# Transposed attention outputs, paired score heads, a transposed first projection and the softmax division on GpSimd, in a hybrid decoder layer with a 32-expert MoE

## The reference: what is computed

```python
h = rms_norm(x, g_mix)
rq, rk, rv, rg, mq, mk, mv, cq, gl = split(h @ w_in)     # 256x256, 256x256, 256x512 ... , 256x3072
o_ret  = rms_norm(retention(rq, rk * 64**-0.5, rv)) * silu(rg)   # 4 heads: causal scores times a decay, no softmax
o_moba = causal softmax attention of mq, mk, mv with ALiBi       # 8 heads of 64, q and k RMS-normed
o_mem  = softmax attention of cq into 256 memory tokens          # 4 heads of 128, keys ck and values cv from mem
y = gates0 * (o_ret @ w_br_ret) + gates1 * (o_moba @ w_br_moba) + gates2 * (o_mem @ w_br_mem)
x = x + y @ w_out
```

## Time and profile before

| | |
|---|---|
| median of 3 runs | 1211.34 us (1210.7 to 1211.85) |
| profiled execution, its own time | 1211.36 us |
| its span, first to last instruction | 1209.5 us |
| mean granted TensorE clock | 0.996 |
| PE busy | 1151.7 us (95%) |
| DVE busy | 410.5 us (34%) |
| ACT busy | 225.6 us (19%) |
| POOL busy | 8.7 us (1%) |
| bytes moved by DMA | 454.93 MB, mean 376 GB/s |

### The profile page before, as it was taken

The page is one execution under the profiler, slowest core; times in us unless marked ns, Lnnn a source line. Parts: engine busy times, 40 slices in busy tenths (PEclk is TensorE's granted clock), DMA queues, the critical chain, the costliest instruction groups (busy, mean ns, idle before and its releaser), DMA issues.

```text
span 1209.5 us, 13242 instructions
## 1 busy us (share of the span) xinstructions
PE 1151.7 (95%) x5401; PEld 536.6 (44%) x5401; DVE 410.5 (34%) x677; ACT 225.6 (19%) x344; POOL 8.7 (1%) x17
## 2 busy tenths in 40 slices
PE   8999999999999999999999999998999999899997
PEld 5888888874333333333433333333333333333332
DVE  4865656864222222222222222222222222222221
ACT  3544447441000000010100000000000000000001
POOL 0100000000000000000000000000000000000000
PEclk9999999999998999999999999999999999999999
DMA  9755454599999999999999999999999999999995
GB/s 352 255 181 169 157 171 157 183 374 429 427 426 423 413 427 429 426 430 424 430 427 429 427 428 428 427 428 429 427 429 427 427 428 430 426 429 426 429 428 237
DMA packets 52322, 454.93 MB, mean 376 GB/s; under 512 B 4368, under 2 KB 4400, under 8 KB 27504
## 3 DMA queue, kind: packets, MB, share of 16 engines
q1 hardware_dynamic: 50816, 449.69, 89.8%
q0 software_dynamic: 784, 2.38, 0.5%
q10 hardware_dynamic: 672, 2.10, 0.5%
HBM read 453.11 MB, written 1.05 MB: 375 GB/s over the span
## 4 chain that ended last, share of the span: by engine, by line
PE 58%; DMA 40%; DVE 1%; issue 1%; ACT 0%; SPq 0%; DVEq 0%; ACTq 0%
PE PS L1456 19%; DMA merge_raw<-in_w_mlp 14%; DMA prob_raw<-in_w_mlp 14%; DMA raw<-in_w_mlp 12%; PE PS L1462 9%; PE PS L1273 6%; PE PS L1275 5%; PE PS L1274 5%; PE PS L1492 3%; PE PS L1431 2%; PE PS L1290 1%; PE PS L1269 1%; PE PS L1438 1%; PE PS L1344 1%; PE PS L1444 1%
## 5 line engine op out<-in xcount | busy, mean ns | idle before, releaser
L1456 PE MATMUL PS<-raw,XG 128*64 128x512 f32 x544 | 123.0, 594 | 11.2 <-DMA raw<-in_w_mlp 11.2
L1185 DVE TENSOR_SCALAR hT<-PS 128x512 f32<-128x512 f32 x32 | 22.1, 692 | 317.7 <-PE PS L1456 317.7
L779 ACT ACTIVATE hT<-hT 128x512 f32<-128x512 f32 x31 | 19.5, 630 | 553.0 <-DVE hT L1185 553.0
L1456 PE MATMUL PS<-merge_raw,XG 128*64 128x512 f32 x480 | 107.5, 596 | 6.2 <-DMA merge_raw<-in_w_mlp 5.9
L857 DVE TENSOR_TENSOR rest<-raw,mix_hi 128x2048 fp32r<-128x2048 f32 x38 | 87.0, 2291 | 55.2 <-ACT mix_hi L631 55.2
L1116 DVE COPY XG<-PS 128x512 f32<-128x512 f32 x32 | 22.1, 692 | 229.0 <-PE PS L1438 229.0
L1123 DVE TENSOR_TENSOR X<-X,PS 128x512 f32<-128x512 f32 x120 | 74.4, 682 | 53.1 <-PE PS L1492 53.1
L1273 PE MATMUL PS<-mix_hi,hTh 128*128 128x512 f32 x224 | 89.8, 401 | 0.0
L1275 PE MATMUL PS<-mix_hi,hTl 128*128 128x512 f32 x224 | 88.2, 394 | 0.0
L1274 PE MATMUL PS<-rest,hTh 128*128 128x512 f32 x224 | 88.1, 393 | 0.0
L631 ACT ACTIVATE mix_hi<-raw 128x2048 fp32r<-128x2048 f32 x38 | 72.6, 1913 | 42.9 <-PE PS L1275 39.9
(11 more groups left out here) (272 smaller groups left out, 1246.8 us busy)
## 6 DMA issues: line engine op xcount, KB each, us to landing
raw<-in_w_mlp SPq DMA_DIRECT2D x48, 2048.0 KB, 34.1
merge_raw<-in_w_mlp SPq DMA_DIRECT2D x47, 2048.0 KB, 33.8
gate_raw<-in_w_mlp SPq DMA_DIRECT2D x24, 2048.0 KB, 32.5
value_raw<-in_w_mlp SPq DMA_DIRECT2D x24, 2048.0 KB, 32.7
hi_raw<-in_w_mlp SPq DMA_DIRECT2D x24, 2048.0 KB, 32.3
prob_raw<-in_w_mlp SPq DMA_DIRECT2D x24, 2048.0 KB, 33.8
raw<-in_w_in SPq DMA_DIRECT2D x24, 1024.0 KB, 5.1
raw<-in_w_mem_kv SPq DMA_DIRECT2D x4, 1024.0 KB, 5.1
```

The costliest lines, as they stand in the source:

```text
L1185: dve.tensor_scalar(glu, PS[:, 0:1024:2], LIMIT, None, ALU.min).then_inc(swi, 1)
L1456: mm = pe.matmul(PS[h * SL:(h + 1) * SL, n * 512:(n + 1) * 512], XG[:, 2 * u + c, :], tile[:, cols], start=False, stop=(u == W1U - 1 and c ...
```

## The change

- **First group transposed.** `rqk` now holds 128 x 128 blocks of the weights still and streams the 256 tokens of `hTf` by, with k in the outer loop and the four output blocks in the inner one, into four banks (0, 1, 4, 5). DVE copies q^T and k^T straight out; the `qT` tasks of `rqk` go. The row scale of x, which had been multiplied into q and k, is left off q and squared into the scale of `rv`; the retention norm takes a per-token epsilon in two square roots on ACT in place of one.
- **Scores in row halves.** `ret_s` and the moba `sc` treat two heads together, one in rows 0 to 63 of the array and one in rows 64 to 127, alternating matmul by matmul. The first 128 queries no longer get scores for keys 128 to 255, so `alibi`, the maxima and exp run over 128 + 256 columns; the maxima are negated by the reduction itself.
- **Softmax division on GpSimd.** POOL multiplies the probabilities in place by the reciprocals, two `tensor_scalar` instructions for a head, and `pT` waits for that (`norm_done`) and no longer for exp.
- **Outputs transposed.** `pv` holds V still and streams the transposed probabilities by, so it makes o^T: one task for two moba heads (each in half of the columns) or one mem head. ACT copies out the high part and DVE the remainder; the `oT` tasks of moba and mem go.
- Several SBUF tiles move, the second bias load and the router's loads on POOL come behind the first multiplications, and `b_mlp2` no longer waits for `oT`.

```diff
@@ rqk and its readers
-               "mq": tasks(*[("qT", "rqk", t) for t in tiles]),
+               "mq": [],
-                        for t in range(TT):
-                            ins = dve.tensor_scalar(tq[0][:, t, :], P2[:, t, :], rx[:, t:t + 1], None, ALU.mult)
+                        dve.tensor_tensor(rx_sq[:, :], rx, rx, ALU.mult).then_inc(rx_sq_done, 1)
+                        for c in (0, 2):
+                            b = RQK_BANKS[c]
+                            ins = dve.tensor_copy(qTs[g][:, c:c + 2, :],
+                                                  PS[:, 512 * b:512 * b + 1024].rearrange("p (c n) -> p c n", c=2)[:, :, 0:S])
+                    if g == "rqk":
+                        for k in range(KC):
+                            w = raw[k // 4][:, :].rearrange("p (k n) -> p k n", k=4)[:, k % 4, :]
+                            if k in PIECE_AT:
+                                pe.wait_ge(hTf_done, PIECE_AT.index(k) + 1)
+                            if k < 3:
+                                pe.wait_ge(first_w[k], 16)
+                            if k in (4, 6):
+                                pe.wait_ge(second_w[(k - 4) // 2], 16)
+                            for c in range(4):
+                                mm = pe.matmul(banks[RQK_BANKS[c]][:, 0:S], w[:, c * P:(c + 1) * P], hTf[:, k, :],
+                                               start=(k == 0), stop=(k == KC - 1))
@@ POOL
+            def normalised(h):
+                if HEADS[h][0] == "moba":
+                    pool.wait_ge(rcp_done, h + 1)
+                else:
+                    in_sbuf(pool, ("sc", h))
+                for it in range(TT):
+                    cols = SCORE_COLS[it] if HEADS[h][0] == "moba" else slice(it * S, (it + 1) * S)
+                    ins = pool.tensor_scalar(probs[h % 4][:, cols], probs[h % 4][:, cols], smx[:, 3, 2 * h + it:2 * h + it + 1], None, ALU.mult)
+                ins.then_inc(norm_done, 1)
...
-            for i in range(6):
+            for i in range(7):
                 if i == 2:
                     load_router(pool)
+                if i >= 1:
+                    normalised(2 * i - 2)
+                    normalised(2 * i - 1)
                 if i >= 2:
                     pool.wait_ge(pair_sem(f"gate{i - 2}"), GI[f"gate{i - 2}"] // 2 + 1)
+                if i == 6:
+                    continue
                 pool.dma_start(bg[:, i % 2, :], a["b_gate"][0:1, 512 * i:512 * i + 512].to_broadcast([P, 512])).then_inc(bias_in[i % 2], 16)
@@ ACT
-                        roots(f"ret{hp}", 2 * TT, RET_DV)
+                        head_roots(f"ret{hp}", 2, RET_DV)
+                    elif kind == "pv":
+                        br, c = key[1:]
+                        act.wait_ge(task_done, TASKS[key] + 1)
+                        act.activation(oTp[br][0][:, c, :], b[:, 0:S], ACT.Copy).then_inc(part_high, 1)
@@ DVE
-                        dve.scalar_tensor_tensor(src, alibi[:, :], 2.0 ** (-8.0 * (hh + 1) / MOBA_H), b, ALU.mult, ALU.add)\
+                        dve.scalar_tensor_tensor(src[:, 0:384], alibi[:, :], 2.0 ** (-8.0 * (hh + 1) / MOBA_H), b[:, 0:384], ALU.mult, ALU.add)\
+                        for it in range(TT):
+                            dve.tensor_reduce(smx[:, 1, 2 * h + it:2 * h + it + 1], src[:, SCORE_COLS[it]], AX.X, ALU.max, negate=True)\
+                                .then_inc(max_done, 1)
-                    dve.tensor_tensor(o[br][:, :, hh * hd:(hh + 1) * hd],
-                                      b[:, 0:TT * hd].rearrange("p (t d) -> p t d", d=hd),
...
+                    dve.wait_ge(part_high, PARTS.index(key) + 1)
+                    dve.tensor_tensor(oTp[br][1][:, c, :], b[:, 0:S], oTp[br][0][:, c, :].bitcast(F32), ALU.subtract).then_inc(done, 1)
@@ PE
+                    if br == "moba":
+                        pe.wait_ge(bank_read[(n + 1) % 4], (n + 1) // 4)
+                        heads = [(slice(64 * i, 64 * i + 64), bank(("sc", h + i))) for i in range(2)]
+                        for it in range(TT):
+                            for rows, sc in heads:
+                                mm = pe.matmul(sc[:, SCORE_COLS[it]], qTs[gq][rows, h // 2, it * P:(it + 1) * P],
+                                               qTs[gk][rows, h // 2, 0:(it + 1) * P], start=True, stop=True)
...
-                    pe.wait_ge(exp_done, 2 * h + 2)
+                    pe.wait_ge(norm_done, h + 1)
...
+                    for jt in range(TT):
+                        q0 = P * jt if br == "moba" else 0
+                        for i, a in enumerate(heads):
+                            h = HEADS[a][1]
+                            mm = pe.matmul(b[i * hd:(i + 1) * hd, q0:S], V[vg][:, jt, h * hd:(h + 1) * hd],
+                                           PT[a % 4][:, jt * S:jt * S + S - q0], start=(jt == 0), stop=(jt == 1))
```

More of the change, by code:

```diff
@@ L86, with out_block @@
 SLOTS = ["mv", "rg"] + [f"gate{i}" for i in range(6)]
+def out_block(a):
+    br, h = HEADS[a]
+    return (br, h // 2) if br == "moba" else (br, h)
 def schedule():
@@ L164 @@
          "posi", "gi", "bsel", "it"]
-PARTS = [s[1:] for s in schedule() if s[0] == "task" and (s[1] in ("oT", "yT"))]
+PARTS = [s[1:] for s in schedule() if s[0] == "task" and s[1] in ("pv", "oT", "yT")]
 RI = {n: i + 1 for i, n in enumerate(ROUTE)}
@@ L281, in build @@
         mix = ExitStack()
-        oTp = {br: [sb(f"oT_{br}{p}", [P, 4, S], F32R, scope=mix) for p in range(2)] for br in ("moba", "ret", "mem")}
+        oT_homes = {(br, p): sb(f"oT_{br}{p}", [P, 4, S], F32R, scope=mix)
+                    for br, p in (("moba", 0), ("ret", 0), ("unused", 0), ("mem", 0), ("mem", 1), ("ret", 1))}
         mem = sb("mem", [P, TT, D], scope=mix)
@@ L1256, in _ @@
                         w = raw[m % MIX_RING][:, :].rearrange("p (k n) -> p k n", k=4)
-                        if t == 0 and g not in NATIVE_GROUPS:
+                        if t == 0:
                             pe.wait_ge(wl_done, SPLIT_UNITS.index(m) + 1)
@@ L1286, in _, with transposes @@
                     pe.wait_ge(bank_read[n % 4], n // 4)
-                def transposes(src, rows=P, blocks=4):
+                def transposes(src, blocks=4):
                     for c in range(blocks):
-                        mm = pe.transpose(b[0:P, c * P:(c + 1) * P], src(c), ident)
+                        mm = pe.transpose(b[:, c * P:(c + 1) * P], src(c), ident)
                     return mm
-                if kind == "qT" and key[1:] == ("rqk", 0):
+                if kind == "qT" and key[1:] == ("mq", 0):
+                    pe.wait_ge(pair_sem("rqk"), 1)
                     pe.wait_ge(const_in, 16 * N_CONST)
@@ L1300, in _ @@
                     h = key[1]
-                    po, c = 64 * (h % 2), h // 2
-                    q, k = qTs["rqk"][po:po + 64, c, :], qTs["rqk"][po:po + 64, 2 + c, :]
-                    for t in range(TT):
-                        in_sbuf(pe, ("qT", "rqk", t))
-                    pe.matmul(b[:, 0:S], k[:, 0:P], q, start=True, stop=True)
-                    mm = pe.matmul(b[:, S:384], k[:, P:S], q[:, P:S], start=True, stop=True)
+                    if h % 2:
+                        continue
+                    pe.wait_ge(pair_sem("rqk"), 1)
+                    pe.wait_ge(bank_read[(n + 1) % 4], (n + 1) // 4)
+                    heads = [(slice(64 * i, 64 * i + 64), bank(("ret_s", h + i))) for i in range(2)]
+                    q, k = qTs["rqk"][:, h // 2, :], qTs["rqk"][:, 2 + h // 2, :]
+                    for rows, sc in heads:
+                        pe.matmul(sc[:, 0:S], k[rows, 0:P], q[rows, :], start=True, stop=True)
+                    for rows, sc in heads:
+                        mm = pe.matmul(sc[:, S:384], k[rows, P:S], q[rows, P:S], start=True, stop=True)
+                    mm.then_inc(task_done, 2)
+                    continue
                 elif kind == "ret_o":
@@ L1342, in _ @@
-                    for c, (it, jt) in enumerate(order):
-                        last = c + 1 == len(order) or order[c + 1][0] != it
-                        mm = pe.matmul(b[:, it * hd:(it + 1) * hd], PT[h % 4][:, c * P:(c + 1) * P], V[vg][:, jt, hh * hd:(hh + 1) * hd],
-                                       start=(jt == 0), stop=last)
+                    br, c = key[1:]
+                    vg = "mv" if br == "moba" else "cv"
+                    heads = [a for a in range(NH) if out_block(a) == (br, c)]
@@ new lines, in _ @@
+                    for a in heads:
+                        in_sbuf(pe, ("pT", a))
+                    pe.wait_ge(pair_sem(vg), GI[vg] // 2 + 1)
+                    hd = MOBA_HD if br == "moba" else MEM_HD
+                    for jt in range(TT):
[4 more added lines that the diff above has]
+                                           PT[a % 4][:, jt * S:jt * S + S - q0], start=(jt == 0), stop=(jt == 1))
```

143 lines of the change are left out of this document (62 added, 81 removed).

## The result

The changed kernel takes **1216.7 us** (median of 5 runs, 1214.23 to 1218.01) against 1210.81 for the kernel before in the same job (5 runs, 1210.58 to 1211.85): ratio 1.0044, 95% interval 1.0029 to 1.0059. It is slower by 5.9 us; the forecast was 1205.9, 5.4 less than before, and the range ended at 1210.0. The profiled execution took 1216.7 with a span of 1214.6.

The account below looks back on a forecast made before the run. PE was taken to bound the kernel until the weight stream starts at 245.6 us, saturated DMA after. Gains of 7.4 less POOL stalls of 1.8 and 0.1 left 5.5, giving 1205.9 us; range 1202.5 to 1210.0.

Parts of the forecast that it names:

- What bounds the kernel: Ahead of the expert weight stream's start at 245.6 us, a microsecond taken from PE moves the end by a microsecond.
- p: POOL's time to multiply one moba head's probabilities: 0.75 us taken, between 0.51 and 1.05; 1.0 for a mem head.
- slot 1: First attention slot, without cover: PE stalls for POOL by 0.3 + 2p, put at 1.8 us (1.3 to 2.4).
- 2p - 1.6: PE's stall for POOL in each of slots 2 to 4 when 2p exceeds 1.6; 0.1 us put in all.
- slot 6, called covered: Two pv of mem stand ahead of the transposes on PE (1.79 us), said to cover POOL's multiplies.
- rival C: Attention slots: a POOL multiply costs over 0.65 us on average, p over 1.3, making the kernel slower; chance 0.07.
- The gain: PE time saved ahead of the weight stream by all parts, before POOL's stalls: 7.4 us (5.0 to 9.2).
- pv and sc: Moba slots on PE: scores and outputs for head pairs each save 0.4 us a pair, 1.6 each for four.
- First group: rqk at the start: 1.3 us from the new order filling a load wait, 0.87 from eight dropped transposes.
- oT, ret_s, pv of mem: PE in attention: dropped output transposes save 1.74 us, paired retention scores 0.2, mem outputs 0.1.
- D: Rival: POOL multiplies and DVE's rest hold each other up at SBUF, time 1211 to 1217; chance 0.03.
- E: Rival: the gain doesn't reach the end because the first item's start sets the MoE part, about 1211.3; chance 0.03.

Follow-up runs that it names:

- e1: The changed kernel with the softmax division left out, so POOL multiplies nothing and results are wrong: 1207.17 us, ratio 0.9967.
- e4: The changed kernel with a slot's exponentials and sums ahead of its weight split, POOL keeping the division: 1207.78 us, ratio 0.9971.
- e2: The changed kernel with the four division multiplies of a slot on DVE in place of POOL: 1208.61 us, ratio 0.9979.
- e3: The changed kernel with 17 and 10 unused transposes on PE in slot 1 while it waits for POOL: 1214.98 us, ratio 1.0030.
- e6: The changed kernel with sums ahead of the split, division on DVE and pv tasks behind pT on PE: 1205.48 us, ratio 0.9954.
- e8: The kernel before with only the first group transposed and no other part of the change: 1210.60 us, ratio 1.0000.
- e11: The kernel before with one unused tile of 8 bytes a partition behind eps2: 1211.73 us, ratio 1.0006.
- e10: e8 with ten warm-up matmuls in place of eight and rx_sq 64 bytes long: 1207.60 us, ratio 0.9969.
- e13: The kernel before with one unused tile of 64 bytes a partition behind eps2: 1208.08 us, ratio 0.9979.
- e9: e6 with ten warm-up matmuls in place of eight and rx_sq 64 bytes a partition where it was 8: 1202.91 us, ratio 0.9930.
- e12: The changed kernel with rx_sq 64 bytes a partition where it was 8: 1214.82 us, ratio 1.0035.

## Why the prediction was wrong

- **What bounds the kernel**: right. Span less start was 963.1 to 964.0 in the changed kernel and e1 to e4, and every gain or loss ahead of the stream came out at the end.
- **The step that failed is POOL's price**: p = 0.75 was taken, between the clears' 0.51 and 1.05 as its upper bound; it is 1.5, and 1.8 where 1.0 was taken. The bound doubled the clears' price, while a multiply costs three times theirs, and nothing in the trace supported the factor of two. With p = 1.5 the prediction's own formulas give 3.3 in slot 1 (measured 2.94), 2p - 1.6 = 1.4 in slots 2 to 4 (0.82 each) and about 1.4 in slot 5 (1.17); slot 6, called covered, waited 0.57. By these formulas the waits are 8.9 and the change is 1.5 slower, where 7.1 of waits and 5.9 slower were measured: the price alone turns the sign and leaves the range, but not the whole loss is price. The case is rival C, whose point was p = 1.3, at 0.07. e2 (engine) and e4 (cover) take most of this loss away (1.4 and 0.6 are left over e1), so price and lack of cover are shown.
- **A cost that wasn't in the sum**: the granted clock behind slot 1's waits, 3.3 us in the trace. The stall was priced as idle time alone. The rows show the clock fall, and in e3's trace, with PE work in the waits, it doesn't; the medians of e3 give 1.7 for it, within the noise.
- **The gain was put too high**: 7.4 was forecast, 5.0 at the least; e1, with nothing of POOL's, got 5.4 in its trace, its fastest execution, and 3.6 in the medians. The points on pv and sc, the first group and oT say where it went, as far as is known.
- **The Trainium skill** was right in its direction. "GPSIMD Engine Reference" calls the engine the wrong choice for elementwise work in its opening, ahead of section 1, and the traces agree: 2.99 on POOL, 1.01 on DVE. The two rates of its section 3.1 gave p of 1.05 and 0.78; measured was 1.5, and the measurement decides.
- **pv and sc**: 0.8 a slot predicted, 0.78 in e6. But in the change as made one slot kept only 0.16 of it (e1): 0.40 goes to the bank that DVE empties late, the rest to slower `pT` and scores beside it. The prediction asked whether DVE's `rest` would be late next, not whether the pair's second bank was free.
- **First group**: 1.3 + 0.87 predicted. Against kernels with the same offsets, each taken against its own job, it brought 0.9 (e8 against e11) and 1.0 (e10 against e13), in medians that are good to about 1 us. PE entered the next group 0.96 earlier (19.57 in e10, 20.53 in e13), not 1.3: the load wait of 2.04 in the row of before, which the step builds on, is 1.54 and 1.43 in e11 and e13, and the first `rest`, taken as fixed at 20.37, was done at 19.50 in the changed kernel. e10's trace shows where the rest stays: in the loads of the next groups. The prediction saw that the first `rest` hangs on a DMA; the same holds two groups on.
- **oT, ret_s, pv of mem**: 2.04 predicted, not tried by themselves. e9 against e13, both with 64 bytes, is 5.6 for the whole change when nothing stalls (8.1 and 2.4 below the kernel before in their jobs); 1.0 for the first group and 4 x 0.78 leave 1.5 for these. That is a remainder and not a measurement.
- **Tile positions**: not thought of. `rx_sq`'s 8 bytes cost 0.8 by e11, which is within its noise, and 64 bytes alone gain 2.4 (e13).
- **Rivals D and E**: neither showed in the changed kernel. There no multiply met `rest`, as the prediction argued, and the end moved with the stream. In e4 two multiplies did meet it and were held until it was done (2.85 and 2.81 for 0.91). The rule that the prediction quotes for D from the Trainium skill, "SBUF — State Buffer", section "Who interferes with whom", agrees with these two records.

The ledger of the changed kernel at the stream's start, from the traces: 5.4 gained (e1), less 7.1 of waits, 3.3 of clock and 0.5 of first group, makes 5.5 lost; measured 5.8. In the medians it is 3.6 gained and 9.5 lost to the division, which makes 5.9.

The best version is e9: sums first, division on DVE, `pv` behind `pT`, two more warm-up matmuls, 64 bytes: 0.9930 (0.9916 to 0.9943), 8.1 us faster than the kernel before. 2.4 of these go with the 64 bytes, which need nothing of the change.

## What to carry to other kernels

An operation that moves to an engine for which the trace has no row of that kind needs an upper bound at several times its nearest row, and the plan needs cover for that bound or an order that makes it (here, sums ahead of the split). Look then at what the covered work now runs beside: in e4 two multiplies tripled in length beside `rest`, and only the cover kept that from costing. Price a stall on TensorE with what may follow it: in the changed kernel's trace 2.9 us of waits were followed by another 3.3 of slow clock. And when a tile is added, compare the mean matmul of an untouched group before and after; if that moved, the allocation is part of the result.

## What the runs showed of the hardware

- A one-input `tensor_scalar` in f32 on POOL takes 595 ns for 128 elements a partition and 913 for 256; DVE does two of each in 1.01 us.
- TensorE's granted clock fell to 0.50 while PE was in 1.98 and 0.96 us of waits with three transposes between them, and came back some 6.5 us later; in e12, with 2.15 and 0.96, some 3.5 us later. After one wait of 1.0 (e2) it did not fall.
- Early in an execution records can take 628 ns (e8) for 379 later, where the page's clock row shows no fall; with two more warm-up matmuls they took 390 (e10). Five of nine traces with the transposed group and eight warm-up matmuls start slow, none of three with ten; that is too few to call the warm-up the cause.
- A POOL `tensor_scalar` that started 0.24 us behind a DVE `tensor_tensor` with two inputs in SBUF took 2.85 us for 0.91 and ended 0.80 after it; the DVE instruction kept its 2.29 (e4).
- The position of tiles in SBUF moved matmul records between 390 and 395 ns and whole groups between 5.44 and 5.60 us. Which property of the position does it is open: 8 and 64 bytes were the only shifts tried.
